# Moving the slot bookkeeping behind the activations in an expert loop

## The reference

```python
logits = (h @ w_router + b_router).astype(jnp.float32)
top_val, top_exp = lax.top_k(logits, TOP_K)            # TOP_K = 4 of 32 experts
gate_w = jax.nn.softmax(top_val, axis=-1)
...
gt = jnp.minimum(xb @ w_gate[e] + b_gate[e], 7.0)
up = jnp.clip(xb @ w_up[e] + b_up[e], -7.0, 7.0)
y  = (gt * jax.nn.sigmoid(1.702 * gt) * (up + 1.0)) @ w_down[e] + b_down[e]
```

## Time and profile before

| | before |
|---|---|
| median of 3 runs | 1668.96 us (1668.53 to 1672.62) |
| the profiled execution | 1668.53 us, span 1666.4 us |
| PE busy | 1394.5 us (84%) |
| DVE busy | 798.7 us (48%) |
| ACT busy | 198.9 us (12%) |
| POOL busy | 284.6 us (17%) |
| DMA, hardware queue, share of 16 engines | 72.7% |
| DMA, software queue (gathers and scatters) | 5.0% |

### The profile page before, as it was taken

One profiled execution on the slowest core, in us unless ns is written; L12 is line 12 of the kernel. 1 busy time (PEld: TensorE's weight loads), 2 busy tenths in 40 slices (PEclk: granted clock), 3 DMA queues, 4 the chain that ended last, 5 costly groups with the idle time before them and its releaser, 6 DMA issues. The chain is left out here.

```text
span 1666.4 us, 38740 instructions
## 1 busy us (share of the span) xinstructions
PE 1394.5 (84%) x13037; PEld 571.5 (34%) x13038; DVE 798.7 (48%) x2816; ACT 198.9 (12%) x522; POOL 284.6 (17%) x217
## 2 busy tenths in 40 slices
PE   6999988889839885778886998897999996969683
PEld 3444454454423321222221343232333331323221
DVE  1129675554964521424442554454455553525344
ACT  1011255550010000000000000000000000000002
POOL 0000000013512210111111221121122221212111
PEclk8999979999959976779897999798899997979896
DMA  9821066724284999999999889789989969496994
GB/s 345 210 76 51 1 218 217 246 92 177 78 314 157 401 408 413 407 408 409 404 361 412 301 315 406 308 321 393 403 316 405 387 233 405 126 407 223 405 410 147
DMA packets 161041, 488.14 MB, mean 293 GB/s; under 512 B 39791, under 2 KB 58283, under 8 KB 143596
## 3 DMA queue, kind: packets, MB, share of 16 engines
q1 hardware_dynamic: 144876, 470.84, 72.7%
q0 software_dynamic: 16128, 16.82, 5.0%
HBM read 474.40 MB, written 17.76 MB: 295 GB/s over the span
## 5 line engine op out<-in xcount | busy, mean ns | idle before, releaser
L1044 PE MATMUL banks<-arena,misc 128*32 128x512 f32 x5248 | 671.7, 642 | 174.3 <-DMA arena<-in_w_up 166.4
L1044 PEld LDWEIGHTS banks<-arena,misc 128*32 128x32 f32 x5248 | 164.5, 114 | 575.2 <-DMA arena<-in_w_up 309.0
L1054 PE MATMUL banks<-arena,master 128*32 128x256 f32 x5248 | 329.2, 393 | 4.3 <-DVE master L1703 2.2
L1697 DVE STREAM_TRANSPOSE misc<-misc 128x256 f32<-128x256 f32 x83 | 54.0, 651 | 438.1 <-PE banks L1044 429.3
L1054 PEld LDWEIGHTS banks<-arena,master 128*32 128x32 f32 x5248 | 168.5, 113 | 155.7 <-issue 70.3
L649 POOL DMA_INDIRECT misc<-moe_input,misc x84 | 88.3, 1052 | 729.2 <-DVE misc L1728 686.5
L665 POOL DMA_INDIRECT moe_output<-misc x82 | 130.2, 1587 | 228.5 <-issue 224.7
L1275 ACT ACTIVATE banks<-cst 128x256 f32<-128x256 f32 x82 | 31.8, 388 | 1091.2 <-DVE cst L1785 1091.2
L814 PE MATMUL banks<-arena 128*128 128x512 f32 x256 | 112.6, 595 | 0.0
L1708 DVE TENSOR_SCALAR master<-cbias 128x128 bf16<-128x128 f32 x340 | 95.1, 344 | 13.0 <-issue 8.4
L1747 DVE LOAD_MASK_SELECT banks<-master x84 | 1.2, 14 | 165.1 <-DMA master<-expert_bias 151.1
(11 more groups left out here) (307 smaller groups left out, 1127.5 us busy)
## 6 DMA issues: line engine op xcount, KB each, us to landing
arena<-in_w_gate SPq DMA_DIRECT2D x256, 512.0 KB
arena<-in_w_up SPq DMA_DIRECT2D x256, 512.0 KB
arena<-in_w_down SPq DMA_DIRECT2D x128, 1024.0 KB
arena<-in_w_ada SPq DMA_DIRECT2D x12, 2048.0 KB, 13.1
arena<-in_x SPq DMA_DIRECT2D x2, 2048.0 KB, 8.4
arena<-in_w_in SPq DMA_DIRECT2D x2, 2048.0 KB, 9.7
master<-bias_by_distance SPq DMA_DIRECT2D x16, 256.0 KB, 4.6
arena<-in_w_in SPq DMA_DIRECT2D x8, 256.0 KB, 4.3
```

The costliest lines, as they stand in the source:

```text
L1044: last = nc.tensor.matmul(two(bank[2 * b][strip(j), :]), hTe[:, k, :], arena[:, 24 * b + 2 * k:24 * b + 2 * k + 2, quarter(j)], start=Fals ...
L1054: last = nc.tensor.matmul(bank[2 * b + 1][strip(j), 0:256], actT[:, q, c, :], DN(b, q, c)[:, quarter(j)], start=False, stop=(q == 3 and c ...
L1697: nc.vector.transpose(hTe, xg.rearrange("p (t k) -> p k t", k=KC)).then_inc(s_xe, 1)
```

## The change

In `body` the two calls `moved_on` and `slot_values` are moved from behind the clip of the up half to behind the down bias. They are the same instructions with the same waits.

```diff
@@ body(b, m, here, landed, bias_landed)
                 nc.vector.tensor_scalar(gcl, bank[2 * b][:, 0:256], 7.0, None, ALU.min).then_inc(s_gdr, 1)
                 dve.wait_ge(s_act, m + 1)
                 nc.vector.tensor_scalar(ucl, bank[2 * b][:, 256:512], 7.0, -7.0, ALU.min, ALU.max).then_inc(s_urd, 1)
-                moved_on(m + 2, m + 2, m * 2 + 4, m + 1)
-                slot_values(m + 3, m * 2 + 5)
                 dve.wait_ge(s_gdr, m + 1)
                 dve.wait_ge(s_sig, m + 1)
                 nc.vector.tensor_tensor(gcl, sig, gcl, ALU.mult).then_inc(s_pr, 1)
...
                 nc.vector.scalar_tensor_tensor(gcl, ucl, 1.0, gcl, ALU.add, ALU.mult).then_inc(s_act, 1)
                 activations_transposed(m + 2, m + 1)
                 down_bias(b, bias_landed, m + 1)
+                moved_on(m + 2, m + 2, m * 2 + 4, m + 1)
+                slot_values(m + 3, m * 2 + 5)
                 one_hot(expert_of(ds(m + 3, 1)))
                 scatter_indices(m + 3, landed)
```

## The result

| | before | after |
|---|---|---|
| median of six runs each | 1670.79 us (1668.51 to 1673.38) | 1685.82 us (1681.13 to 1687.54) |
| ratio, 95% interval | | 1.0084 (1.0066 to 1.0100) |
| the profiled execution, its span | 1668.53, 1666.4 us | 1679.86, 1677.7 us |
| PE busy | 1394.5 us | 1398.8 us (83%) |
| DVE busy | 798.7 us | 807.5 us |

The changed kernel is slower: by the ratio 14 us (11 to 17). I had forecast 1672 us, within 1667.5 to 1680, and the time lies outside that range. The kernel before scatters as well, by 4.9 us over its six runs.

A forecast was written before the change was run, and what follows sets the result against it. The pace was taken to pass between TensorE and the weight stream, with the gather hidden. 2.8 us of kept lateness plus 0.4 at the end made 3.2 on 1668.5, lying 0.4 under the median: forecast 1672 us, range 1667.5 to 1680.

The forecast's parts named there:

- The loop: Transpose, indices, gather, landing: gather starts at 5.2 us, full-stream loop takes 11.06 us against the item's 10.64.
- No gain from the activations: Transposed activations come 0.6 us earlier, but TensorE needs them much later, so nothing is gained mid-loop.
- The end: At the loop's end, last scatters 0.2 us later plus 0.1 to 0.3 of late last transpose: 0.4 us in all.
- The rest of VectorE: One_hot, scatter indices, `weighted` and `gate_up_bias` begin about 0.2 us later, against 3.96 us idle: no cost.
- What of it stays: TensorE's delay is lost only if the weight stream then waits for TensorE; over the 82 items 2.8 us stay.
- Rival B: In dense runs of items, the loop costs more than absorption gives back: 1674 to 1681 us, chance 0.27.
- the replay: Lateness carried through 82 items, each with its own landing, item time and DMA share; about 43 transposes late.
- the margin of 1.76: Before the change, gather start 3.04 plus landing 5.84 made 8.88 of the 10.64 us item, leaving 1.76 us unseen.
- The bound: Gather landing 0.3 us sooner loses nothing, 0.3 us later loses 8.8 us.
- my bound at a start of 5.0 us: Gather starting 5.0 us after the transpose instead of 5.2 loses 0.1 us.
- the cover of 0.7 us: On TensorE, L1697 may be about 0.7 us late before the first gate-up matmul that needs it is delayed.

The follow-up runs named there:

- the delay alone: Kernel before in its own order, only the gather held back about 2.2 us by four ScalarE sigmoids; ratio 1.0102, median 1686.67 us.
- the split kernel: Against the kernel before, token sum and gather indices stay behind the up half's clip, other bookkeeping goes behind the down bias; ratio 0.9998.
- place 1: Against the kernel before, both bookkeeping calls stand right behind transpose L1697, ahead of the clips; ratio 0.9999.
- half the weights: Kernels before and after, each reading half of the weight columns for 30 of 32 experts; medians 1436.03 and 1438.22 us.
- the longer item: Kernel before with eight more small matmuls ahead of TensorE's slot matmuls, each item 0.20 us longer; ratio 1.0037.

## Why the prediction was wrong

**The loop, right.** The activations came forward by 0.6 us, the bookkeeping went back, the gather starts 5.19 us after the transpose (forecast 5.2), L1703 stands 2.39 after it (2.4), 44 transposes besides the first are gather-bound (about 43), and the loop closes at 10.9 to 11.1 (11.06). That this, and nothing else of the change, makes the time is shown by the delay alone, and by the split kernel from the other side.

**No gain from the activations, right:** the split and place 1. **The end, right:** 0.4 us forecast; the last item starts 10.9 us later than before (1640.66 against 1629.79) and the span is 11.3 longer, so 0.4. **The rest of VectorE, off without a cost:** one_hot starts 4.73 us after the transpose and not 4.35, as VectorE stands idle for 0.53 us ahead of it, and the scatter behind the gather starts at 7.46 (1023.23 - 1015.77) and not 7.1.

**What of it stays, wrong: this is the step that failed.** I carried the lateness through the items "each with its own landing" of before and kept 2.8 us; the loop of the profiled execution grew by 10.5. Rival B is what came, with a time above even its range of 1674 to 1681: its sign was TensorE idle for L1697 over 10 us in sum, and 10.9 came (17.6 less the 6.7 at the start). Its condition, a loop of 11.2 us on, did not come in the median; single loops of 12 to 13 us did. Three things are in the difference. I redid the replay with numbers of the later traces, so their shares are estimates, not measured one by one:

*1. The landings are not those of before.* In the full stream the median is the same (5.84 and 5.87 us), which is all I had looked at. But before, none took over 6.4 us beside the loop's second, and after, nine took 6.5 to 7.5. Five of the nine (issued at 535.6, 975.9, 1084.2, 1454.7 and 1539.8 us) went out just behind a restart of the weight stream; four more that did took 6.0 to 6.3, so all nine of these lie above the median. In the kernel before the same nine gathers went out 2.2 us earlier, and eight of them landed in 3.0 to 3.7 us. A sixth slow one (1302.9) had a gap in the stream shortly ahead of it, with a DMA share of 0.81 over the 4 us before. The last three (868.0, 1151.2 and 1477.6) had none, with shares of 1.06 to 1.07, took 6.5 to 6.6, and are not explained by a restart. One restart, line by line. In the kernel before, SyncE's issue, GpSimd's and the transpose it feeds:

```profile
533.17 0.64 SPq L460 DMA_DIRECT2D master<-expert_bias  x1
```
```profile
533.17 1.04 POOL L649 DMA_INDIRECT misc<-moe_input,misc  x1 [5.87 <-DVE misc L1728]
```
```profile
540.76 0.65 DVE L1697 STREAM_TRANSPOSE misc<-misc 128x256 f32<-128x256 f32 x1 [3.60 <-PE banks L1044]
```

and its software queue from 533.1 to 536.6 us:

```profile
q0 software_dynamic: 48, 0.13, 14.8%
```

The gather leaves together with the stream's first transfer, its 48 packets are through in 3.4 us, and the transpose isn't concerned. In the changed kernel:

```profile
533.51 0.64 SPq L460 DMA_DIRECT2D master<-expert_bias  x1
```
```profile
535.62 1.10 POOL L649 DMA_INDIRECT misc<-moe_input,misc  x1 [7.20 <-DVE misc L1728]
```
```profile
542.94 0.64 DVE L1697 STREAM_TRANSPOSE misc<-misc 128x256 f32<-128x256 f32 x1 [4.85 <-DMA misc<-moe_input,misc]
```
```profile
543.81 1.50 PE L1044 MATMUL banks<-arena,misc 128*32 128x512 f32 x12 [0.83 <-DVE misc L1697]
```

and from 535.6 to 541.0 us:

```profile
q0 software_dynamic: 35, 0.11, 6.8%
```

The stream's first issue is at 533.51, the gather comes 2.1 us behind it, 35 of its 48 packets are through after 5.4 us, and all land at 7.3. TensorE waits. With after's own landings the replay keeps 7.7 us instead of 2.7. By this estimate it is the largest part.

*2. The start is not always 5.2.* Around 1290 us a gather is held up on GpSimd. VectorE and GpSimd in the changed kernel:

```profile
1285.25 0.65 DVE L1697 STREAM_TRANSPOSE misc<-misc 128x256 f32<-128x256 f32 x1 [3.61 <-DMA misc<-moe_input,misc]
...
1289.33 0.20 DVE L1728 TENSOR_SCALAR misc<-cbias 128x1 f32<-128x1 f32 x1
...
1297.75 0.63 DVE L1697 STREAM_TRANSPOSE misc<-misc 128x256 f32<-128x256 f32 x1 [5.19 <-DMA misc<-moe_input,misc]
...
1310.45 0.63 DVE L1697 STREAM_TRANSPOSE misc<-misc 128x256 f32<-128x256 f32 x1 [5.36 <-DMA misc<-moe_input,misc]
```
```profile
1291.83 1.06 POOL L649 DMA_INDIRECT misc<-moe_input,misc  x1 [8.50 <-DVE misc L1740]
...
1302.88 1.11 POOL L649 DMA_INDIRECT misc<-moe_input,misc  x1 [8.10 <-DVE misc L1728]
```

It starts 2.30 us after the indices are done (1291.83 - 1289.53) instead of 0.94, and the gather after it takes 7.57 us to the next transpose. The two items take 12.50 and 12.70 us, 3.9 us over two items of 10.64, which is more than I gave the whole loop. The trace of before has a hold-up at the same gather of the loop, the 58th:

```profile
1283.90 1.06 POOL L649 DMA_INDIRECT misc<-moe_input,misc  x1 [6.58 <-issue]
```

That gather started 4.40 us after its transpose instead of 3.04, 1.36 late, and the margin of 1.76 hid it. The 58th gather starts 1.35 to 1.40 us late in all thirteen traces, those with half the weights too, and the 41st 0.9 to 1.0 late. In the changed kernel the 41st is this one:

```profile
1084.24 1.05 POOL L649 DMA_INDIRECT misc<-moe_input,misc  x1 [7.96 <-issue]
```

It starts 6.13 us behind its transpose (1078.11) and takes 6.98 to the next one, so that loop took 13.1 us. What holds these two gathers up is open. I had taken the median start. With after's own start times as well the replay keeps 9.7 us.

*3. Less is absorbed, perhaps.* The rest, 0.8 us here and up to 3 in the other traces, I put down to delay that I had let the weight stream absorb; the longer item gives the same sign (0.38 kept, not 0.24). In the trace the loss came between 1066 and 1133 us (2.8, forecast 0.5) and between 1240 and 1342 (5.1, forecast 1.4), with 0.7, 1.5 and 1.2 in three later stretches where I had counted on none; 0.9 came back before the last two items. Before 980 us, where I had kept 0.7, some 0.4 stayed, and around 1215 to 1237, where I had 0.2, nothing. One of the three, in the changed kernel:

```profile
1450.00:1513.00 63.00, 50.08 (x520) 16.61 (x512) 24.70 (x96) 2.36 (x8) 10.80 (x8) 0.81 0.95 367
```

TensorE waits for weights there and the DMA share is 0.95, so a late gather should not count; yet item 71 started 10.0 us later than before (1472.15 to 1482.14) and item 72 10.55 (1502.62 to 1513.17). I read a mean of a stretch as if the stream were full at each moment of it. Part of it needs no gather, though: in the split kernel, which has no late one, the same two items start 1.5 and 2.4 us later than before (1473.62 and 1505.06), and its whole loop is 2.9 us longer than that of before, with a ratio of 0.9998 over all its runs. Two traces can differ by as much, so the size of this third part is not shown.

**The bound.** I bounded the landing by 0.3 us either way as a shift common to all gathers, which gave 8.8 us. What came is a tail on some. And my bound at a start of 5.0 us lost 0.1, where the curve shows 5.2 us lost at 4.82 already, with a median loop of 10.71 us (4.82 + 5.87 + 0.02): the cover of 0.7 us that I gave TensorE did not keep a loop of varying landings from losing.

**Open.** That a gather which is issued into a restart lands late, where one that is issued at its first transfer doesn't, is only seen, in the traces; no run took the restart away, and three slow gathers stand at none. That executions of the changed kernel differ by 6 us (1681.1 to 1687.5) is tied to the number of slow gathers by three traces only, and the kernel before, with none, has runs that differ by 4.9.

## What to carry to other kernels

An operation that nobody waits for has a margin, and the margin is a number: add up the closed loop it stands in across all engines, here transpose, indices, gather, landing, and compare it with the item; 1.8 us were there, and a move of 2.2 us on a queue with 4 us of idle time took more. Judge it by the late landings, not by the median: by the curve the loss began at a start of about 4.6 us (an estimate), with a median loop of 10.49 us that was still shorter than the item. A move that frees nothing on the path (0.6 us of activations nobody awaited) can only spend such a margin.

## What the runs showed of the hardware

The same gather of 128 KB, issued by GpSimd, landed after 2.2 to 3.7 us with no weights in flight or together with their first transfer, and after a median of 5.8 to 5.9 in the full stream. Behind a restart, about 2 us after its first issue, it took 6.0 to 7.4 us in the three traces of the changed kernel. Its own moment of issue thus set its price by about a factor of two. Shifting its start from 3.04 to 5.19 us behind the transpose changed its tail and hardly its median; the kernels with starts of 2.38 and 2.55 us have medians of 5.5 and 5.6. Two gathers of the loop, the 41st and the 58th, start 0.9 to 1.0 and 1.35 to 1.40 us late in each of the thirteen traces; no run shows why.
